# Stationary weight tiles and a 176-token size class in the expert stage of a two-layer trunk

## The reference

```
logits = xf @ w_router                       # (512, 8)
top_vals, top_idx = top_k(logits, 2)
gates = softmax(top_vals)
for each expert e, with the tokens that chose it:
    h = silu(x @ w1[e]) * (x @ w3[e])        # 1024 -> 3584
    y = h @ w2[e]                            # 3584 -> 1024
out[t] = sum over its two experts of gate * y
h = h + out;  result = rms_norm(h, final_g)
```

## Time and profile before

| | |
|---|---|
| median of three runs | 2222.48 us |
| the profiled execution | 2224.46 us |
| its span | 2222.8 us |
| granted clock of TensorE | 0.974 |
| PE busy | 2070.9 us (93%) |
| weight loads of PE | 1708.7 us (77%) |
| DVE busy | 1536.5 us (69%) |
| ACT busy | 1197.4 us (54%) |
| read from HBM | 473.80 MB, 220 GB/s over the span |

### The profile page before, as it was taken

How to read it: one execution, slowest core, us unless ns; L and a number is a source line. 1 busy time by engine, 2 the same in 40 slices (tenths; PEclk the granted TensorE clock), 3 DMA queues, 4 the chain that set the end, 5 groups by cost and what they waited for, 6 DMA issues and landing times.

```text
span 2222.8 us, 30246 instructions
## 1 busy us (share of the span) xinstructions
PE 2070.9 (93%) x9627; PEld 1708.7 (77%) x9628; DVE 1536.5 (69%) x1667; ACT 1197.4 (54%) x1493; POOL 84.3 (4%) x122
## 2 busy tenths in 40 slices
PE   5989999999979996999999999999999998999991
PEld 4767788888867775888788878787888787878881
DVE  6885666666667856665666688896666897876655
ACT  4442555555544423554555577776555776765543
POOL 1000000000000003000000000000000000000002
PEclk9999999999989997999999999999999999999996
DMA  7221866656632214666666699998665999996643
GB/s 228 91 66 38 289 187 187 186 185 189 189 123 95 76 57 143 227 226 208 235 225 221 215 370 374 334 379 307 226 226 196 364 373 331 374 333 226 227 151 128
DMA packets 245647, 489.64 MB, mean 220 GB/s; under 512 B 16564, under 2 KB 86308, under 8 KB 245604
## 3 DMA queue, kind: packets, MB, share of 16 engines
q1 hardware_dynamic: 236288, 461.43, 60.5%
q0 software_dynamic: 7936, 27.03, 3.7%
q10 hardware_dynamic: 1380, 0.61, 0.1%
HBM read 473.80 MB, written 15.22 MB: 220 GB/s over the span
## 4 chain that ended last, share of the span: by engine, by line
PE 87%; DVE 5%; issue 3%; DMA 2%; ACT 1%; POOL 0%; ACTq 0%; DVEq 0%; POOLq 0%
PE PS L1168 85%; PE PS L1419 1%; DMA raw<-in_expert_w 1%; DVE wlo L598 1%; DVE PS L670 1%; PE PS L1185 1%; ACT whi L327 1%; PE PS L1422 1%; DVE OV L631 1%; DMA OV<-in_norm_mix_g 0%; DVE XN L615 0%; POOL SM L1019 0%; DVE OV L794 0%; DMA raw<-y_rows,addr 0%; ACT XN L345 0%
## 5 line engine op out<-in xcount | busy, mean ns | idle before, releaser
L1168 PE MATMUL PS<-whi,XN 128*128 128x512 f32 x3616 | 1125.3, 394 | 9.6 <-DVE XN L807 4.9
L598 DVE TENSOR_TENSOR wlo<-raw,whi 128x1024 fp32r<-128x1024 f32 x882 | 1035.2, 1220 | 138.7 <-ACT whi L327 132.7
L327 ACT ACTIVATE whi<-raw 128x1024 fp32r<-128x1024 f32 x882 | 885.4, 1052 | 106.3 <-DMA raw<-in_expert_w 50.3
L1168 PEld LDWEIGHTS PS<-whi,XN 128*128 128x128 f32 x3616 | 682.6, 189 | 156.3 <-issue 15.5
L1168 PE MATMUL PS<-wlo,XN 128*128 128x512 f32 x2144 | 773.0, 391 | 0.0
L1168 PE MATMUL PS<-XN,whi 128*128 128x512 f32 x1408 | 478.7, 400 | 5.2 <-DVE XN L615 4.7
L1168 PEld LDWEIGHTS PS<-wlo,XN 128*128 128x128 f32 x2144 | 404.9, 189 | 82.9
L1168 PE MATMUL PS<-XN,wlo 128*128 128x256 f32 (+1 forms) x1088 | 341.5, 314 | 0.0
L1168 PEld LDWEIGHTS PS<-XN,whi 128*128 128x128 f32 x1408 | 266.4, 189 | 72.1 <-issue 6.4
L1168 PEld LDWEIGHTS PS<-XN,wlo 128*128 128x128 f32 x1088 | 206.1, 189 | 15.0
L491 ACT ACTIVATE XN<-PS 128x512 fp32r<-128x512 f32 x56 | 33.5, 598 | 192.1 <-PE PS L1422 151.7
(11 more groups left out here) (195 smaller groups left out, 1030.6 us busy)
## 6 DMA issues: line engine op xcount, KB each, us to landing
raw<-in_expert_w SPq DMA_DIRECT2D x672, 512.0 KB, 5.2
raw<-in_ffn_w SPq DMA_DIRECT2D x144, 512.0 KB, 3.7
raw<-in_w_in SPq DMA_DIRECT2D x40, 512.0 KB, 4.7
raw<-in_w_out SPq DMA_DIRECT2D x16, 512.0 KB, 4.2
y_rows<-OV POOLq DMA_DIRECT2D x8, 512.0 KB, 5.3
y_rows<-OV POOLq DMA_DIRECT2D x1, 3072.0 KB, 11.6
RES<-in_x SPq DMA_DIRECT2D x4, 512.0 KB, 5.3
x_tok<-OV POOLq DMA_DIRECT2D x4, 512.0 KB, 2.9
```

The costliest lines, as they stand in the source:

```text
L327: act.activation(whi[:, u0 % CONV, half(h)], raw[:, r, half(h)], ACT.Copy).then_inc(s["hi_done"], 1)
L598: dve.tensor_tensor(wlo[:, w, half(h)], raw[:, u0 % RAW, half(h)], whi[:, w, half(h)].bitcast(F32), ALU.subtract).then_inc(s["lo_done"], 1)
L1168: return pe.matmul(out_, lhsT, rhs, start=start, stop=stop, skip_group_check=True)
```

## The change

`WIN` goes from 192 to 176, so that the high and the low part of all tokens of a heavy visit fit in one PSUM bank side by side (352 of 512 columns). The tokens stand in one tile `XX` (high and low part, 8 x 176 columns each).

Heavy visits: the ups have weight tiles stationary (`heavy_up`), 16 pairs of a 352-column and a 176-column matmul a unit. One output tile of 128 hidden features goes to each of banks 0 to 3, for w1 and then again for w3. ACT copies the low halves out (`low_columns`), DVE adds them (`heavy_sum`), both two banks at a time; ACT takes silu, DVE multiplies (176 columns by four tiles), and the high and low parts are taken without transposes (`heavy_hi`, `heavy_lo`). The seven groups are one loop from the second on, whose down chooses by a branch whether it opens the sum (`group_down`).

Light visits: the first turn's transposes come behind the next group's up of w1 and go to bank 1. In all visits both token transposes (`gT`, `gT_ext`) come ahead of the last down, and four splits move ahead of the copy-out.

The end: the gathers wait for the last tokens' transposes in place of `stream_end` and go to the working tile `OV`; DVE adds one block ahead before it finishes another; ACT writes its squares' scratch into PSUM.

```diff
-WIN = 192
+WIN = 176
-        XH, XL, XE = (XF[:, D * i:D * i + D].rearrange("p (k n) -> p k n", n=P) for i in range(3))
+        XX = XF[:, 0:2 * KD * WIN].rearrange("p (a k n) -> p a k n", a=2, k=KD)
...
 (ACT)
+            def low_columns(i, g, u, part):
+                for p in range(2):
+                    if p == 0:
+                        act.wait_ge(s["up_half"], i * (2 * GROUPS) + g * 2 + (part + 1))
+                    else:
+                        act.wait_ge(s["unit_used"], i * UNITS + g * 6 + (CONV + u))
+                    act.activation(low[:, pair(p), :], PS[:, pair(p), WIN:2 * WIN],
+                                   ACT.Copy).then_inc(s[("w1_low", "w3_low")[part]], 1)
+            def heavy_silu(i, g):
+                for p in range(2):
+                    act.wait_ge(s["w1_sum"], i * (2 * GROUPS) + g * 2 + (p + 1))
+                    act.activation(up1[:, pair(p), :], up1[:, pair(p), :], ACT.Silu).then_inc(s["w1_silu"], 1)
+            def heavy_hi(i, g, used):
+                act.wait_ge(s["h_done"], i * GROUPS + g + 2)
+                act.wait_ge(s["unit_used"], i * UNITS + g * 6 + (CONV + used))
+                act.activation(hidH3, hv[:, :, 0:P], ACT.Copy)
+                act.activation(hidE3[:, :, 0:EXT], hv[:, :, P:WIN], ACT.Copy).then_inc(s["hid_hi"], 1)
...
+                with act.Fori(1, GROUPS - 1) as g:
+                    m_split(i, g, 3, 4)
+                    low_columns(i, g, 0, 0)
+                    heavy_silu(i, g)
+                    m_split(i, g, 5, 6)
+                    low_columns(i, g, 2, 1)
+                    m_split(i, g, 7, 8)
+                    heavy_hi(i, g, 4)
...
 (DVE)
+            def heavy_sum(i, g, part):
+                for p in range(2):
+                    dve.wait_ge(s[("w1_low", "w3_low")[part]], i * (2 * GROUPS) + g * 2 + (p + 1))
+                    dve.tensor_tensor((up1, hv)[part][:, pair(p), :], PS[:, pair(p), 0:WIN], low[:, pair(p), :],
+                                      ALU.add).then_inc(s[("w1_sum", "w3_sum")[part]], 1)
+                if part:
+                    dve.wait_ge(s["w3_sum"], i * (2 * GROUPS) + g * 2 + 2)
+                    dve.wait_ge(s["w1_silu"], i * (2 * GROUPS) + g * 2 + 2)
+                    dve.tensor_tensor(hv, hv, up1, ALU.mult).then_inc(s["h_done"], 1)
...
+                with dve.Fori(1, GROUPS - 1) as g:
+                    m_split(i, g, 3, 4)
+                    heavy_sum(i, g, 0)
+                    m_split(i, g, 5, 6)
+                    heavy_sum(i, g, 1)
+                    m_split(i, g, 7, 8)
+                    heavy_lo(i, g)
...
+                m_split(i, GROUPS - 1, 7, 8, 9, 10)
                 dve.wait_ge(s["y_part"], i + 1)
...
-            dve.sem_inc(s["stream_end"], 1)
+            add_experts(0)
+            for b in range(1, TB):
+                add_experts(b)
+                mean(4 * TB + b - 1)
+                if b > 1:
+                    finish(b - 2)
+            mean(4 * TB + 3)
+            finish(2)
+            finish(3)
...
 (POOL)
-            pool.wait_ge(s["stream_end"], 1)
+            held(s["gT_done"], n_more * 2 + (2 * E + 2))
...
 (PE)
+            def heavy_up(i, g, n0, part, free):
+                for q in range(2):
+                    u = MOE_BASE + n0 + q
+                    w = u % CONV
+                    for t in range(4):
+                        if q == 0 and t % 2 == 0 and free:
+                            pe.wait_ge(s[("w3_sum", "w1_sum")[part]],
+                                       i * (2 * GROUPS) + g * 2 + (2 * part - 1 + t // 2))
                         for kk in range(4):
...
+                            mm(PS[:, t, 0:2 * WIN], whi[:, w, a], XX[:, :, k, :], k == 0, False)
+                            ins = mm(PS[:, t, 0:WIN], wlo[:, w, a], XX[:, 0, k, :], False, k == KD - 1)
+                        if q and t == 1:
+                            ins.then_inc(s["up_half"], 1)
                     ins.then_inc(s["unit_used"], 1)
...
+            def light(i):
                 pe.wait_ge(s["glo_done"], i * 3 + 2)
+                m_up(i, 0, 0, 0)
                 pe.wait_ge(s["glo_done"], i * 3 + 3)
+                m_up(i, 0, 2, 1)
+                pe.wait_ge(s["a_free"], i * GROUPS + 2)
+                m_up(i, 1, -2, 0)
+                m_T(i, 0, 1)
+                m_up(i, 1, 0, 1)
+                pe.wait_ge(s["y_evac"], i * 2 + 4)
+                pe.wait_ge(s["hid_ok"], i * GROUPS + 2)
+                m_down(i, 1, 2, True, False, False)
+                m_T(i, 1, 2)
```

More of the change, by code:

```diff
@@ L126, in build_program @@
         c1c = OV[:, 0:2048].rearrange("p (b n) -> p b n", b=2)
-        sA, hM, sE, hE, tE = (OV[:, GROUP * i:GROUP * i + GROUP] for i in range(5))
+        sA, hM = (OV[:, GROUP * i:GROUP * i + GROUP] for i in range(2))
+        low, up1, hv = (OV[:, 4 * WIN * i:4 * WIN * (i + 1)].rearrange("p (t n) -> p t n", n=WIN) for i in range(3))
         gF = OV[:, 7168:8192]
@@ L515, in visit @@
+            def visit(i, ext):
                 if ext:
-                    gate_ext(i, g, 2)
-                m_split(i, g, 5)
-                hidden_hi(i, g, ext)
+                    heavy(i)
+                else:
+                    light(i)
                 x_split(i + 1)
-                m_split(i, g, 6, 7, 8)
-                if not ext:
-                    for n in ("e_up", "e_gate"):
-                        act.sem_inc(s[n], GROUPS)
+                x_split_ext(i + 1)
+                m_split(i, GROUPS - 1, 7, 8, 9, 10)
@@ new lines, in heavy @@
+            def heavy(i):
+                m_split(i, 0, 5, 6)
+                heavy_sum(i, 0, 0)
+                m_split(i, 0, 7, 8)
+                heavy_sum(i, 0, 1)
+                heavy_lo(i, 0)
+                with dve.Fori(1, GROUPS - 1) as g:
+                    m_split(i, g, 3, 4)
+                    heavy_sum(i, g, 0)
+                    m_split(i, g, 5, 6)
+                    heavy_sum(i, g, 1)
+                    m_split(i, g, 7, 8)
+                    heavy_lo(i, g)
+                g = GROUPS - 1
+                m_split(i, g, 3, 4)
+                heavy_sum(i, g, 0)
+                m_split(i, g, 5, 6)
+                heavy_sum(i, g, 1)
+                heavy_lo(i, g)
@@ L827, in visit @@
-                g = GROUPS - 1
-                if ext:
-                    up_ext(i, g)
-                m_split(i, g, 3, 4)
-                gated(i, g, 2, ext)
-                m_split(i, g, 5)
-                hidden_lo(i, g, ext)
+                    heavy(i)
+                else:
+                    light(i)
                 x_split(i + 1)
-                m_split(i, g, 6, 7, 8)
-                if not ext:
-                    for n in ("e_sum", "e_lin"):
-                        dve.sem_inc(s[n], GROUPS)
+                x_split_ext(i + 1)
@@ L1451, in _, with visit @@
+            def visit(i, ext):
+                if ext:
+                    heavy(i)
+                else:
+                    light(i)
             pe.wait_ge(s["prm_in"], 128)
```

282 lines of the change are left out of this document (138 added, 144 removed).

## The result

| | before | after |
|---|---|---|
| median of the runs, us | 2222.68 (2221.13 to 2223.88, 4 runs) | 2157.78 (2156.64 to 2158.27, 4 runs) |
| ratio, 95% interval | | 0.9708 [0.9696, 0.972] |
| profiled span, us | 2222.8 | 2155.8 |

A forecast was written before the change was run, and what follows sets the result against it. TensorE was taken to bound the kernel (93% busy), with light visits level with the weight stream. Terms -31.1, +3, -10.5, -2.8, +1, -16 and -3.9 sum to -60.3 us, giving 2162 us; own range 2150 to 2176, 80% range 2120 to 2190.

The forecast's parts named there:

- Part 1: Heavy ups with weights stationary: a 352- and 176-column pair takes 0.280 us, limited by weight load, transposes gone; -31.1 us.
- Part 2: Heavy groups' turn between w1 and w3, now sharing four banks: new wait just fits, 0.1 us a turn; +3 us.
- slow-turn rival: Between w1 and w3, sums come behind queued splits: PE waits about 3.7 us, 28 times; 2263 us, chance 7%.
- Part 3: Heavy visits' first turns and ends: no wait for transposes -10.5 us, ends -2.8, first visit's extra columns +1.
- forecast of +1 us for the first visit: First heavy visit must wait for the extra columns before its first matmul; +1 us.
- Part 4: Light visits: later first transposes cover stalls, a little of the end stall goes too; -16 us, bounds 6 and 24.
- My term for PE: Light visits: stalls, half clock and end waits that PE could save, 12.1 us a pair.
- cap of 9.2 us a pair: Light visits: 89.7 MB a pair at 371 GB/s takes 241.8 us against 251, so 9.2 us saved at most.
- My sign of light visits of 119 to 122 us: Sign that the forecast is right: light visits take 119 to 122 us with clock 1.00.
- Part 5: Kernel's end: DVE's last stage falls from 20.9 to about 16.1 us, extra splits cost +0.9; -3.9 us.
- no load limit: Rival for heavy ups: weight load does not limit, a pair takes 0.253 us; 2122 us, chance 10%.
- light visits on DMA: Rival: light visits stay with the DMA and a heavy pair takes 0.286 us; 2183 us, chance 13%.

The follow-up runs named there:

- the last kernel: Changed kernel with token tiles 192 floats apart and, in heavy first turns, one split ahead of the w1 sums; 2146.88 us, 0.9662.
- low64: Changed kernel with the low-tile matmul of the heavy ups over 64 columns in place of 176, low products of tokens 64 to 175 left out; 2229.38 us, 1.0026.

## Why the prediction was right, step by step

**Part 1** was right in its mechanism and 14 us too small. I took 0.280 for the pair; it measured 0.272, and 0.008 x 64 x 28 = 14. The term that was too large is the narrow matmul. In the dense pair it is 0.353 - 0.227 = 0.126, in the new one 0.114: 12 ns of the 33 that I had between the bounds, and I had counted 6. In all, the groups gave 28 x (28.10 - 26.52) = 44.2 us, of which I had 28.1 in parts 1 and 2 together. The 16 between them are the 14, the 3 of part 2, and 1.4 back, since a down took 9.12 and not 9.07. The Trainium skill (TensorE: Matmul & The Clock Gate, section LDWEIGHTS) gives 107 ns for that load. The run with 64 columns bears out that it is the load, and its size is 7 ns off (114); part 1 by that rule, -54, missed the 44 by 10, mine, -31, by 13. What I had announced for a single start, 110 to 118 ns behind a 176-column matmul, is not there: the record has 81 ns, and the rest on the matmul ahead of it (191 in place of 158).

**Part 2** was right: 0.27 us to spare at the turn where I had 0.2, and no stall in the loop at all, so 0 in place of +3. The slow-turn rival had the order of events right and the sizes wrong.

**Part 3** failed; it is the step that went wrong. I had written that with no transposes there is nothing to wait for, -12.3 us with the ends. The four heavy visits gained 43.6, less than their groups' 44.2, so starts and ends together gave nothing. The wait for transposed hidden values (2.2 us, four times) and one half clock did go. But the first turn has the new wait of part 2 as well, and I had worked that out only inside the loop, where the splits have their weights. Behind a light visit they do not: 3.2 and 3.4 us, with 3.4 us at half clock behind each. These come to 3.2 + 3.4 + 2 x 1.7 = 10 us of the 12.9 that the part missed; the rest I have not placed. The forecast of +1 us for the first visit was right: PE waits 2.4 us there for the low part of the extra columns, where it waited 1.5. I had asked for what is late next in part 2 and not here.

**Part 4** came out right, 18.2 against 16, in part by luck. My term for PE, 12.1 us a pair or 24 in all, was good: the light visits gave 18.2, and 24.0 with the tiles 192 apart. Two things came between. One is the distance of the token tiles, 5.8 us, which I had not counted. The other is the cap of 9.2 us a pair, which was too low and happened to stand where that cost brought the gain. The rate in it was no ceiling: the stream ran at 379 GB/s in after, 387 in the last kernel and 390 with less PE work. And my visits of 123 and 128 us were stretches that I had cut short; from transposes to transposes the pair took 255.5:

```profile
1258.73:1514.23 255.50, 246.20 (x1114) 203.15 (x1113) 218.50 (x204) 190.79 (x206) 8.27 (x10) 0.99 0.97 352
```

That is 89.9 MB, at 371 GB/s 242.4 us, so even by my own rate 13.1 us a pair were free, not 9.2. My sign of light visits of 119 to 122 us was met by the second of each pair (121.6) and missed by the first (125.0). The edit that I credited, the later first turn, is worth 6.6 us alone and 9.8 on top of the old end order, and half of the 24 has no experiment behind it.

**Part 5** was right: 4.8 us where I had 3.9; the DVE stage was 16.5 us against 16.1, and putting its order back cost 5.6.

The sum of parts was -60.3 and the span shrank by 67.0. The 6.7 between them are 16 more from the groups, 13 less from the starts and ends, 2 more from the light visits, 1 more from the end and 0.5 ahead of the first visit. So the total is nearer than its parts: the error of part 3 took back most of that of parts 1 and 2. The rivals with no load limit and with light visits on DMA were both refused by the trace (pair 0.272; 379 GB/s), and the visits stayed eight.

## What to carry to other kernels

A stationary operand that changes with every matmul costs its load, here 114 ns for 128 columns, however few columns follow: count a matmul as the larger of the two, and read a pair's sum, not a single start. When a new wait is added to a loop, work it out again for the loop's first turn, with the queues as the stage before leaves them. A change of a tile's width also changes the distance between tiles; test the two apart.

## What the runs showed that I had not expected

- After a stall, 352- and 64-column matmuls in turn stayed at 1.2 GHz for 51 to 65 us, with PE busy throughout (clock 0.50 in the windows of low64), and in the first visit the clock came back 2 us behind the first 512-column matmul of the down (the half clock ends at 929.5):

```profile
927.41 0.26 PE L1236 MATMUL PS<-XN,wlo 128*128 128x64 f32 x1
927.47 1.20 PE L1236 MATMUL PS<-whi,XN 128*128 128x512 f32 x2
928.47 1.05 PE L1236 MATMUL PS<-wlo,XN 128*128 128x512 f32 x2
929.33 1.16 PE L1236 MATMUL PS<-whi,XN 128*128 128x512 f32 x4
```

  With 352 and 176 columns it was back after 3.4 us, in the same place of the program. So less work made this kernel 72 us slower. Without a stall ahead the same pairs ran at 2.4 GHz. What it is in the pairs that keeps the clock down was not tested.
- Tiles 176 floats apart (in place of 192) as stationary operand made a 512-column matmul take 232 ns in place of 227 in a run of them; as moving operand the same tiles cost hardly anything (a group's ups 17.41 us against 17.32).
- The weight stream of one core moved up to 390 GB/s over 80 us (DMA share 1.04), and each of its transfers had waited for DVE to free a buffer, so that is not shown to be its limit.
